# A two-layer diffusion trunk on one core: the opening's modulation rows in four column tiles, the shift row formed inside the first pair of units

## The reference

```python
m = jnp.split((sc @ w_mod[i] + b_mod[i])[:, None, :], N_MOD, axis=-1)    # latents; mc from silu(c_ctx) for the context
h = h + 0.5 * m[2] * _swiglu(_modulate(_rmsnorm(h, ffn1_norm[i]), m[0], m[1]), ffn1_w1[i], ffn1_w3[i], ffn1_w2[i])
# _modulate(n, shift, scale) = n * (1.0 + scale) + shift
```

## Time and profile before

| | us |
|---|---|
| median of three runs (lowest, highest) | 2977.95 (2972.64, 2978.53) |
| the profiled execution, its own time | 2978.58 |
| span of the profile | 2976.8 |
| TensorE busy | 2895.1 (97%) |
| VectorE busy | 1661.0 (56%) |
| ScalarE busy | 890.2 (30%) |
| mean granted TensorE clock | 0.99 |
| L690, all three products, TensorE | 851.0 + 847.8 + 847.4 |
| first `w_mod` loads | 2 x 4096 KB, 18.5 to landing (median) |

### The profile page before, as it was taken

How to read it: one execution, slowest core, us unless ns; L and a number is a source line. 1 busy time by engine, 2 the same in 40 slices (tenths; PEclk the granted TensorE clock), 3 DMA queues, 4 the chain that set the end, 5 groups by cost and what they waited for, 6 DMA issues and landing times.

```text
span 2976.8 us, 43751 instructions
## 1 busy us (share of the span) xinstructions
PE 2895.1 (97%) x16914; PEld 2473.9 (83%) x16914; DVE 1661.0 (56%) x3086; ACT 890.2 (30%) x1389; POOL 104.9 (4%) x82
## 2 busy tenths in 40 slices
PE   7999999999989999999999999999999999999998
PEld 3888888888756788888888888888888757898996
DVE  3877578743366568766777335443433466543443
ACT  4221122233346442211222322122233256422222
POOL 0000000024000000000000000000024000000000
PEclk9999999999999999999999999999999999999999
DMA  5434343422300033433442123222222300233232
GB/s 200 127 120 132 94 127 122 125 55 65 88 1 1 22 99 121 131 108 113 129 128 89 57 63 113 67 61 63 68 71 65 81 1 1 78 92 99 85 101 69
DMA packets 422727, 255.39 MB, mean 86 GB/s; under 512 B 25985, under 2 KB 418025, under 8 KB 422634
## 3 DMA queue, kind: packets, MB, share of 16 engines
q1 hardware_dynamic: 422634, 254.13, 28.7%
HBM read 252.01 MB, written 2.10 MB: 85 GB/s over the span
## 4 chain that ended last, share of the span: by engine, by line
PE 93%; DVE 2%; ACT 2%; issue 1%; DMA 1%; SPq 0%; DVEq 0%; ACTq 0%
PE pair L690 55%; PE pair L686 26%; PE pair L886 2%; PE pair L934 2%; PE pair L646 2%; PE pair L902 1%; PE pair L596 1%; PE pair L911 1%; PE pair L862 1%; ACT buf L1196 1%; PE pair L844 1%; PE pair L919 1%; DMA pro_w<-in_w_mod 0%; DVE n_lo L1355 0%; DVE lo_w L1316 0%
## 5 line engine op out<-in xcount | busy, mean ns | idle before, releaser
L690 PE MATMUL pair<-n_hi,hi_w 128*128 128x258 f32 (+2 forms) x3456 | 851.0, 327 | 14.2 <-DVE n_lo L1355 8.7
L690 PE MATMUL pair<-n_lo,hi_w 128*128 128x258 f32 (+2 forms) x3456 | 847.8, 326 | 0.0
L690 PE MATMUL pair<-n_hi,lo_w 128*128 128x258 f32 (+2 forms) x3456 | 847.4, 326 | 0.0
L690 PEld LDWEIGHTS pair<-n_hi,hi_w 128*128 128x128 f32 x3456 | 538.9, 191 | 74.7 <-issue 10.3
L690 PEld LDWEIGHTS pair<-n_lo,hi_w 128*128 128x128 f32 x3456 | 539.2, 191 | 56.6
L690 PEld LDWEIGHTS pair<-n_hi,lo_w 128*128 128x128 f32 x3456 | 539.1, 191 | 56.1
L1316 DVE TENSOR_TENSOR lo_w<-raw_w,hi_w 128x1024 fp32r<-128x1024 f32 (+1 forms) x296 | 396.7, 1340 | 307.5 <-ACT hi_w L1004 306.7
L1004 ACT CAST hi_w<-raw_w 128x1024 fp32r<-128x1024 f32 (+1 forms) x296 | 328.7, 1111 | 671.6 <-PE pair L690 378.4
L1476 DVE SCALAR_TENSOR_TENSOR mod_acc<-mod_w,silu_c,mod_acc 128x256 f32<-128x256 f32 x896 | 364.6, 478 | 0.0
L1399 DVE TENSOR_TENSOR buf<-pair,rstd 128x512 f32<-128x512 f32 (+1 forms) x308 | 164.7, 570 | 319.1 <-PE pair L690 319.1
L686 PE MATMUL pair<-h_hi,hi_w 128*128 128x512 f32 x1232 | 338.7, 345 | 0.0
(11 more groups left out here) (182 smaller groups left out, 2088.1 us busy)
## 6 DMA issues: line engine op xcount, KB each, us to landing
raw_w<-in_ffn_w SPq DMA_DIRECT2D x176, 512.0 KB, 3.8
mod_w<-in_w_mod SPq DMA_DIRECT2D x64, 1024.0 KB, 5.1
raw_w<-in_ffn_w SPq DMA_DIRECT2D x64, 704.0 KB, 4.6
raw_w<-in_w_in SPq DMA_DIRECT2D x38, 512.0 KB, 3.9
pro_w<-in_w_mod SPq DMA_DIRECT2D x2, 4096.0 KB, 18.5
raw_w<-in_w_out SPq DMA_DIRECT2D x16, 512.0 KB, 4.0
x_tok<-in_x SPq DMA_DIRECT2D x4, 512.0 KB, 5.2
out<-x_tok SPq DMA_DIRECT2D x4, 512.0 KB, 2.7
```

The lines of the kernel that those rows point to most:

```text
L690: mm = pe.matmul(pair[s][:, a:a + m], wt[:, k * P:(k + 1) * P], src[:, of(k):of(k) + m], start=opens, stop=closes)
```

## The change

Four edits, all in or around the opening.

1. *Loads.* Chunk 1 (scale) is loaded first, in two halves of 2 MB with a semaphore each; then the first two weight tiles; then chunk 0 (shift), also in halves; then `mod_w`.
2. *Rows in four column tiles.* `silu_wide` holds for each k the 2 columns of silu(c) padded with zeros to 32. Matmul k writes PSUM partitions 32j to 32j+31 with j = k mod 4, so the row lies as four partial sums in 128 partitions. It is copied whole (128 x 1024), and `mod_columns(m)` folds and turns it at once: 8 matmuls with 128 x 128 of the row as weights and 2 columns of `fold` streaming.
3. *The shift row inside the first pair.* Ahead of the pair only the scale row is formed. `opening_pair` runs the 512-wide parts of both units, with the shift row's matmuls put in at k = 6; then the shift's columns, then `sum_stream`, then the 256-wide parts of both units with the shift columns. The squares and their additions are spread over the normalization, `rstd` is made behind it, and the lambda work is split into `lam_first` and `lam_last` and moved behind it as well.
4. *Shift columns, in all sweeps.* The low part of the shift goes to two more columns of `n_hi`. The second stream is 260 wide for hi x hi, 256 for hi-weight x lo-input, 258 for lo-weight x hi-input. The bias becomes a sum over two column pairs (and for the queries of the differential attention one more instruction for the factor).

```diff
-            wm = t["w_mod"][0].rearrange("(k p) c -> p k c", p=P)
-            for m, dst in enumerate((pro_w1, pro_w2)):
-                sp.dma_start(dst[:, :].rearrange("p (k c) -> p k c", k=KD), wm[:, :, m * D:(m + 1) * D])\
-                  .then_inc(pro_full[m], 16)
+            def load_first_mod(m, dst):
+
+                wm = t["w_mod"][0].rearrange("(k p) c -> p k c", p=P)
+                for k in range(0, KD, KD // 2):
+                    sp.dma_start(dst[:, k * D:(k + KD // 2) * D].rearrange("p (k c) -> p k c", c=D),
+                                 wm[:, k:k + KD // 2, m * D:(m + 1) * D]).then_inc(pro_full[m][k // (KD // 2)], 16)
+
+            load_first_mod(1, pro_scale)
...
                     load_unit(w, 0, 1, True)
+                if q == 0:
+                    load_first_mod(0, pro_shift)
...
             def first_mod(m, src):
                 pe.wait_ge(silu_ready, 2)
-                pe.wait_ge(pro_full[m], 16)
-                for a in range(0, D, 512):
-                    for k in range(KD):
-                        mm = pe.matmul(pair[m][0:2, a:a + 512], silu_c[:, 2 * k:2 * k + 2],
-                                       src[:, k * D + a:k * D + a + 512], start=(k == 0), stop=(k == KD - 1))
+                for r in range(2):
+                    pe.wait_ge(pro_full[m][r], 16)
+                    for a in range(0, D, 512):
+                        for j in range(4):
+                            k = 4 * r + j
+                            mm = pe.matmul(pair[2][32 * j:32 * (j + 1), a:a + 512], silu_wide[:, 32 * k:32 * (k + 1)],
+                                           src[:, k * D + a:k * D + a + 512], start=(r == 0), stop=(r == 1))
...
+            def mod_columns(m):
+                for u in range(KD):
+                    mm = pe.matmul(pair[2][:, 2 * u:2 * u + 2], mod_rows[m][:, u * P:(u + 1) * P], fold[:, 0:2],
+                                   start=True, stop=True)
...
-                        for a, m, of in streams(w, s):
+                        for n, (a, m, of) in enumerate(streams(w, s, 0 if src is src_lo else 2 if wt is lo else 4)):
+                            if part not in (None, n):
+                                continue
...
+            def opening_pair(w):
+                open_slot(w, 0, 0, True)
+                for n in range(KD + LAG):
+                    if n < KD:
+                        pe.wait_ge(n_ready, n + 1)
+                        row(w, n, 0, 0)
+                    if n == LAG:
+                        open_slot(w, 0, 1, True)
+                    if n == KD - 2:
+                        pe.wait_ge(mod_out, 1)
+                        first_mod(0, pro_shift)
+                    if n >= LAG:
+                        row(w, n - LAG, 1, 0)
+                mod_columns(0)
+                pe.wait_ge(cols_out, 1)
+                sum_stream(norm_width(w))
+                pe.wait_ge(shift_ready, 1)
+                for s in range(2):
+                    for k in range(KD):
+                        row(w, k, s, 1)
...
@@ ScalarE, norm_x of the opening
+                        high(0, w_cols)
+                        high(1, w_cols)
+                        split_hi(w, 0, 1, True)
+                        for k in range(2, KD):
+                            high(k, w_cols)
+                            if k in (3, 4, 5):
+                                square_x((k + 2) // 2, k % 2, TOK)
+                        act.wait_ge(mrow_done, 2)
+                        act.copy(mod_rows[0], pair[2][:, :]).then_inc(mrow_out[0], 1)
+                        act.wait_ge(mod_out, 2)
+                        shift_high(w)
...
@@ VectorE, norm_x of the opening
+                    for k in range(3):
+                        add_x(k // 2, k % 2, TOK)
+                    dve.wait_ge(mrow_done, 1)
+                    dve.tensor_copy(mod_rows[1], pair[2][:, :]).then_inc(mrow_out[1], 1)
+                    first_columns(1)
+                    scales(w)
                     split_lo(w, 0, 0)
+                    for k in range(KD):
+                        low(k, w_cols)
+                        if k == 1:
+                            split_lo(w, 0, 1)
+                        if 1 <= k < KD - 3:
+                            add_x((k + 2) // 2, k % 2, TOK)
+                    lam_first()
+                    first_columns(0)
+                    shift_low(w)
+                    mod_add(w, 0, 0, KD)
+                    wait_rstd()
+                    lam_last()
...
-                    dve.tensor_copy(bias[s][:, :], bias_cols).then_inc(pair_free[s], 1)
+                    dve.tensor_reduce(bias[s][:, :], bias_cols, AX.X, ALU.add).then_inc(pair_free[s], 1)
```

More of the change, by code:

```diff
@@ L176, in mods_before @@
     first = next(w["base"] for w in plan_sweeps() if w["layer"] == L and w["what"] == "in")
-    return 1 + sum(1 for v in plan_sweeps() if v["base"] < first and mod_tile(v) is not None)
+    return 2 + sum(1 for v in plan_sweeps() if v["base"] < first and mod_tile(v) is not None)
 def late_rows(w):
@@ L256, in build @@
         proj, v_mla = overlay(("proj", T_IN * TOK, F32), ("v_mla", (TOK // P) * 256, F32))
[L257 to L260, removed]
+        x_tok, pro_shift, c_rows, rows, lam_row, silu_wide = overlay(
+            ("x_tok", (TOK // P) * D, F32), ("pro_shift", KD * D, F32), ("c_rows", P, F32), ("rows", 3 * P, F32),
+            ("lam_row", DEPTH * 4 * DDIM, F32), ("silu_wide", KD * 32, F32))
+        mod_rows = [x_tok[:, m * D:(m + 1) * D] for m in range(2)]
+        lam_prod = x_tok[:, 2 * D:2 * D + TOK]
         h_hi = sb("h_hi", FG * TOK, F32R)
@@ L278, in build @@
         x_full = sem("x_full")
-        pro_full = [sem("pro_full0"), sem("pro_full1")]
+        pro_full = [[sem(f"pro_full_shift{r}") for r in range(2)],
+                    [sem(f"pro_full_scale{r}") for r in range(2)]]
         cols_done = sem("cols_done")
@@ L394, in blocks, with streams, shift_cols @@
             return lat + [(1, SEQ, CTX, lambda k: k * BLK)] * (n == TOK)
-        def streams(w, s):
+        def streams(w, s, extra):
             lead = 0 if w["ctx"][s] else CTX
-            return ((lead, BLK - lead, lambda k: k * BLK + lead), (BLK, 258, lambda k: KD * BLK + k * TAIL))
-        def shift_cols(tensor):
-            return tensor[:, KD * BLK:KD * BLK + KD * TAIL].rearrange("p (k c) -> p k c", c=TAIL)[:, :, 256:258]
+            return ((lead, BLK - lead, lambda k: k * BLK + lead), (BLK, 256 + extra, lambda k: KD * BLK + k * TAIL))
+        def shift_cols(part):
+            return n_hi[:, KD * BLK:KD * BLK + KD * TAIL].rearrange("p (k c) -> p k c", c=TAIL)\
+                [:, :, 256 + 2 * part:258 + 2 * part]
         def out_of(p, n):
@@ L675, in turn_diff, with row @@
                 mm.then_inc(turned_diff, 1)
-            def row(w, k, s):
+            def row(w, k, s, part=None):
                 down = w["what"].endswith("_down")
@@ L1076, in norm_x @@
                 if w is not None and w["base"] == 0:
-                    act.wait_ge(mrow_done, 1)
-                    act.copy(mod_rows[0:2, 0:D], pair[0][0:2, :]).then_inc(mrow_out[0], 1)
-                    shift_high(w)
-                    for k in range(KD):
-                        high(k, w_cols)
-                    cnt["n"] += KD
+                    act.wait_ge(lam_ready, 1)
+                    act.activation(lam_exp[:, :], lam_sum[:, :], ACT.Exp).then_inc(lam_ready, 1)
             def finish(w, i, s):
@@ L1304, in _, with lam_first @@
-            dve.wait_ge(lam_ready, 2)
-            for L in range(DEPTH):
-                link(dve.tensor_tensor(neg_lam[:, L:L + 1], lam_exp[:, 2 * L + 1:2 * L + 2], lam_exp[:, 2 * L:2 * L + 1],
-                                       ALU.subtract))
-                link(dve.tensor_scalar(neg_lam[:, L:L + 1], neg_lam[:, L:L + 1], -LAM_INIT[L], None, ALU.add))
-                g = L * G_LAYER + G_SUB
-                link(dve.tensor_scalar(sub_gain[:, L:L + 1], gains[:, g:g + 1], 1.0 - LAM_INIT[L], None, ALU.mult))
+            def lam_first():
+                link(dve.tensor_copy(lam_prod[:, 0:512], pair[3][:, 512:1024]))
+                lv = lam_prod[:, 0:512].rearrange("p (l two d) -> p l two d", two=2, d=DDIM)
+                products = lam_prod[:, 512:768].rearrange("p (l d) -> p l d", d=DDIM)
+                dve.tensor_tensor(products, lv[:, :, 0, :], lv[:, :, 1, :], ALU.mult).then_inc(cols_out, 1)
+                dve.wait_ge(cols_out, 1)
+                dve.tensor_reduce(lam_sum[:, :], products, AX.X, ALU.add).then_inc(lam_ready, 1)
@@ new lines, in lam_last @@
+            def lam_last():
+                dve.wait_ge(lam_ready, 2)
+                for L in range(DEPTH):
+                    link(dve.tensor_tensor(neg_lam[:, L:L + 1], lam_exp[:, 2 * L + 1:2 * L + 2], lam_exp[:, 2 * L:2 * L + 1],
+                                           ALU.subtract))
```

(9 more changed lines are left out.)

76 lines of the change are left out of this document (34 added, 42 removed).

## The result

The changed kernel takes 2946.22 us (median of four runs, 2945.51 to 2949.34) against 2978.24 us (2972.64 to 2978.78) for the kernel before: ratio 0.9899, 95% interval 0.9882 to 0.9916. That is 32 us faster, where 9.9 were forecast: outside the range, which ended at 2963. The two profiled executions took 2946.31 and 2978.58 us, with spans of 2944.5 and 2976.8: 32.3 us to be found.

A forecast was written before the change was run, and what follows sets the result against it. TensorE, busy 97% of the span, was taken as the bound; only the second pair's second unit counted, moving from 93.6 to 83.7 us. 2978.6 less 9.9 gave 2968.7 us, range 2964 to 2972, widened to 2963 to 2976.

The forecast's parts named there:

- Shift columns 4, 2, 0: Second streams in all sweeps: 774 columns per k either way, so 0, within 3 us either way.
- What would show it: List of signs: rows of 3.5 to 4.5 us, first weight matmul near 35, widths 256, 258 and 260 within 3 ns.
- k = 4 begins: First pair of the opening: VectorE delivers the fifth input block, k = 4, at 44.6 us.
- shift columns done (C): First pair of the opening: TensorE ends the shift row, seven rows of matmuls and the shift's columns at 61.8 us.
- Order of loads: Start of the opening: scale chunk's second half lands at 26.2 us; weight tiles, shift chunk and their casts stay hidden.
- Four tiles: Modulation rows in the opening: 32 passes, four at a time, take 4.3 us instead of 13.84; bounds 3.5 and 13.9.
- one after another: Rival for the modulation rows: tiles do not overlap, a row takes 13.9 us, 2986 us in all; chance 0.07.
- The first pair: Opening's first two units: VectorE's deliveries pace TensorE, k = 4 and 5 run at 1.2 GHz, shift columns end at 61.8 us.
- VectorE behind C: After the shift columns: VectorE's chain takes 11.05 us, TensorE idles 2.3, then half clock loses 3.4; second unit at 83.7.
- From there the same timeline: Sign: after the second pair's second unit the old timeline repeats; wrong if later sweeps grow by more than 3 us.
- full clock and four tiles at 3.5 us: Rival for the opening: full clock granted everywhere, a row takes 3.5 us, gain 14, 2964 us; chance 0.13.
- The reduction for the bias: VectorE's bias copy (0.14 us) becomes a small reduction: 0 to 0.28 us more per unit, hidden; taken as 0.

## Why the prediction was wrong

**The step that failed** is "Shift columns 4, 2, 0": "0, within 3 us either way". It measured 15.9 us alone, and about 16 by the starts of the matmuls in the changed kernel. The step counted columns (774 either way) and took the nearly equal durations of the forms for equal cost. Neither gives the cost. The 282 ns of a 258-wide stream are the duration of one matmul, and the next one starts 117.5 ns after it; the 289 ns are of 256-wide *first* streams in layer 1, some of them behind a wait, and no second stream of the kind that the change makes. What prices a width is the time from start to start, and the chain of the kernel before had a row that does so, the down projections, whose streams are 512 and 256 wide:

```profile
545.63 80.28 PE pair L686 x462
```

80.28/77 is 1042.6 ns a k, where 178.27/168 is 1061.1 with three streams of 258. Six columns less went with 18.5 ns less, while a column costs 0.47 ns by the difference of the two streams (236 and 117.5 ns, 254 columns), 3 ns for six. By the single starts it is there too the 512-wide stream that is shorter, 229.5 for 236. Times 1304 values of k, 18.5 ns are 24 us: that was the range that an edit of the widths should have been given. Where in it 260, 256, 258 would fall, no row before tells, and the runs put it at 16. The step's own bound was too small even on its own terms: "1728 matmuls of each kind at up to 2 ns" is 3.5 us for one kind and 10.4 for the three, and the 3 ns that "What would show it" allowed make 15.6.

**Terms of the opening**, forecast and measured:

| term | forecast | measured |
|---|---|---|
| a row in four column tiles | 4.3 | 3.6 |
| scale row done | 28.6 | 28.19 |
| first weight matmul | 35.4 | 34.90 |
| k = 4 begins | 44.6 | 43.31 |
| shift columns done (C) | 61.8 | 58.8 |
| idle for `lo_w` | 2.3 | 2.40 |
| second pair's second unit | C+21.9 | C+20.9 |
| the same, absolute | 83.7 | 79.70 |
| gain of the opening | 9.9 | 13.9 |

- *Order of loads*: right. TensorE took the second half up at 26.27 (forecast landing 26.2), and the rest was hidden; only mod_w's second load left a small wait (1.12 us) on VectorE, off the path.
- *Four tiles*: the mechanism was right and the size at the favourable bound. 1.92 us for half a row, 3.57 to 3.64 for a whole one inside the pair, against 8 x 0.434 = 3.5 for complete overlap. The estimate worked out from the Trainium skill's table ("TensorE: Matmul & The Clock Gate", "Why this matters for your kernels"), 4.4, was too slow, the arithmetic of the passes was better. The rival "one after another" was priced nearly rightly: 18.2 us beyond the forecast, 19.4 measured beyond the changed kernel.
- *The first pair*: C came 3.0 us earlier. k = 4 was early by 1.3, the shift row shorter by 0.7, the shift's columns 1.84 for 2.2; the clock came back from 0.50 to full at about 46.4, in the middle of the slow rows that had been allowed to 49.7, which is the other 0.7.
- *VectorE behind C*: idle and its releaser as forecast, to 0.1 us (the terms written down add up to C+10.99 and an idle of 2.4, not C+11.05 and 2.3). The second unit starts at C+20.9 and not C+21.9, mostly because the slow stretch was the short one of the two that were considered (1.7 us lost, not 3.4). The half-clock stretch of the row at 849 came here as well, 3.4 us long behind 2.40 of idle, where the Trainium skill ("TensorE: Matmul & The Clock Gate", "Why this matters for your kernels") puts the limit at idle gaps over about 3 us. The trace disagrees with that limit, since this fall came behind a shorter wait. But that the fall came was partly luck: in the same trace TensorE waited 2.54 us up to 787.96 and 2.50 us up to 828.56, and the clock stayed at 1.00 for the next 6 us both times. One row with a fall didn't make it certain.
- *"From there the same timeline"*: wrong, for the reason above. The test named for it, that the later sweeps would have *grown* by more than 3 us, looked at one side only; they shrank by 16.
- *The rival "full clock and four tiles at 3.5 us"* (gain 14) matches the opening's 13.9 in size by luck: the tiles ran at 3.6, but the clock was not full.
- *The reduction for the bias*, 0: right (0.15 for 0.14).

**What stays open** is why the sequence of widths matters. Shown: with the same matmuls and the same sum of columns, exchanging 256 and 258 costs 10 to 17 ns a k, 1.7 to 2.8 us in a sweep of 168; most of that (12 of 17 ns) is in the start-to-start time of the 512-wide streams, and in the last up sweep of layer 1 the gain is in streams of 256 (three of the six that took 120 ns take 117.0 to 117.6, one takes 122.6); the streams start at the same columns of `n_hi`, `n_lo` and `pair` in all these kernels, so the start address within a tile is not what differs; and the same sweep of the same matmuls can run at 1048 in one kernel and at 1054 in another, each for the whole sweep. Argued only: that something periodic in TensorE's or its memory's timing meets the widths, since the numbers gather at steps of 6.7 ns without keeping to them. No run here separates that.

## What to carry to other kernels

Where one matmul form is issued thousands of times, no edit of its width is free: look for another place in the same trace where the form has the other width, compare the two from start to start, multiply the difference by the count, and give the range that product, not zero. The mean duration of one matmul isn't its cost. Keep products with different widths in the order that a measurement favours, and re-measure after any change of width, since column counts didn't predict it here. A reordering of an opening should be priced with and without the faster piece that it relies on: here the order without the column tiles would have lost 5.5 us.

## What the runs showed of the hardware that was not expected

- Six fp32r streams of one k (512 and a narrow one, three times) took, by narrow widths in order of issue: 256, 256, 256 1041 ns; 260, 256, 258 1048 or 1054; 260, 256, 256 1050; 258, 256, 256 1054; 260, 256, 260 1054; 258, 258, 258 1061; 260, 260, 260 1061 (1051 in some sweeps); 260, 258, 256 1064 (1058 in one sweep of the kernel with the other order of matmuls). With a first stream of 256 in place of the 512 the order is another: 260, 256, 256 took 707 and 256, 256, 256 712.
- Four column tiles of 32 with 128 rows of fp32 each overlap almost fully: 16 passes of 512 columns in 1.92 us at full clock and 3.64 at 1.2 GHz, where one after another each pass takes 13.92/32 = 0.435 at full clock.
- An idle of 2.40 us was followed by 3.4 us at 1.2 GHz, likewise with 2.48; waits of 2.50 and 2.54 us in the changed kernel's mixer of layer 0 were not.
